# First weights split in halves and a reordered start in a two-layer hybrid decoder trunk

## The reference

```
for l in range(2):
    h = rmsnorm(x, norm_mix[l])
    u, sq, sk, sv, dq, dk, dv, gate_logits = split(h @ w_in[l])
    y_ssm = GLU(gelu(s5_ssm(u, ssm_lam_re[l], ssm_lam_im[l], ssm_log_dt[l], b, c, d)))
    y_sb  = stick_breaking_attention(sq, sk, sv)
    y_da  = differential_attention(rope(dq), rope(dk), dv)
    x = x + (sum of sigmoid(gates) * branch projections) @ w_out[l]
    x = x + cross_attention(rmsnorm(x), rmsnorm(mem)) @ w_xo[l]
    x = x + square(relu(rmsnorm(x) @ w_up[l])) @ w_down[l]
return rmsnorm(x, norm_final)
```

## Time and profile before

| | |
|---|---|
| three runs | 1027.1 us median (1026.31 to 1028.13) |
| the profiled execution | 1026.68 us, its span 1025.0 us |
| TensorE matmul busy | 990.7 us, 97% of the span |
| TensorE weight load busy | 877.4 us, 86% |
| VectorE busy | 765.7 us, 75% |
| ScalarE busy | 550.5 us, 54% |
| mean granted clock | 0.998 |
| HBM read | 176.67 MB |

### The profile page before, as it was taken

One profiled execution on the slowest core, in us unless ns is written; L12 is line 12 of the kernel. 1 busy time (PEld: TensorE's weight loads), 2 busy tenths in 40 slices (PEclk: granted clock), 3 DMA queues, 4 the chain that ended last, 5 costly groups with the idle time before them and its releaser, 6 DMA issues. The chain is left out here.

```text
span 1025.0 us, 17644 instructions
## 1 busy us (share of the span) xinstructions
PE 990.7 (97%) x6784; PEld 877.4 (86%) x6784; DVE 765.7 (75%) x1185; ACT 550.5 (54%) x843; POOL 46.2 (5%) x104
## 2 busy tenths in 40 slices
PE   6999999999999999999999999999999999999996
PEld 6977899999897888888889779999988878888885
DVE  5988997888765866889765569787887567666665
ACT  7455436475755645544464663545656565444543
POOL 5004000000000004000000110000000000000000
PEclk9999999999999999999999999999999999999999
DMA  8797438556644666686657853465665446666661
GB/s 330 240 187 181 124 104 268 147 169 182 182 145 123 247 187 185 195 222 190 195 145 203 178 149 100 142 197 149 180 181 167 141 127 188 191 193 189 185 190 78
DMA packets 64163, 181.37 MB, mean 177 GB/s; under 512 B 19728, under 2 KB 21776, under 8 KB 63440
## 3 DMA queue, kind: packets, MB, share of 16 engines
q1 hardware_dynamic: 63648, 179.91, 60.6%
q10 hardware_dynamic: 432, 0.32, 0.1%
HBM read 176.67 MB, written 3.54 MB: 176 GB/s over the span
## 5 line engine op out<-in xcount | busy, mean ns | idle before, releaser
L1288 DVE TENSOR_TENSOR s_w_lo<-s_raw,s_w_hi 128x1024 fp32r<-128x1024 f32 x312 | 374.9, 1228 | 95.4 <-ACT s_w_hi L914 91.6
L914 ACT ACTIVATE s_w_hi<-s_raw 128x1024 fp32r<-128x1024 f32 x312 | 320.8, 1054 | 183.1 <-PE p_T L1876 76.7
L1874 PE MATMUL p_T<-s_hT,s_w_hi 128*128 128x256 f32 x576 | 165.8, 288 | 0.7 <-ACT s_w_hi L914 0.7
L1875 PE MATMUL p_T<-s_hT,s_w_hi 128*128 128x256 f32 x576 | 162.9, 283 | 0.0
L1876 PE MATMUL p_T<-s_hT,s_w_lo 128*128 128x256 f32 x576 | 162.8, 283 | 0.0
L1874 PE MATMUL p_A<-s_w_hi,s_bT_hi 128*128 128x512 f32 x320 | 125.1, 391 | 2.5 <-DVE s_bT_lo L1288 2.5
L1876 PE MATMUL p_A<-s_w_hi,s_bT_lo 128*128 128x512 f32 x320 | 124.7, 390 | 0.0
L1875 PE MATMUL p_A<-s_w_lo,s_bT_hi 128*128 128x512 f32 x320 | 124.6, 389 | 0.0
L1874 PEld LDWEIGHTS p_T<-s_hT,s_w_hi 128*128 128x128 f32 x576 | 110.2, 191 | 4.6 <-issue 2.7
L1875 PEld LDWEIGHTS p_T<-s_hT,s_w_hi 128*128 128x128 f32 x576 | 110.3, 192 | 0.1
L1876 PEld LDWEIGHTS p_T<-s_hT,s_w_lo 128*128 128x128 f32 x576 | 110.3, 192 | 0.0
(11 more groups left out here) (269 smaller groups left out, 1844.1 us busy)
## 6 DMA issues: line engine op xcount, KB each, us to landing
s_raw<-in_weights SPq DMA_DIRECT2D x312, 512.0 KB, 3.7
s_bt<-in_ssm_bt SPq DMA_DIRECT2D x2, 1024.0 KB, 7.3
s_gates<-f_turn SPq DMA_DIRECT2D x16, 128.0 KB, 7.5
s_x<-in_x SPq DMA_DIRECT2D x1, 1024.0 KB, 10.0
s_dv<-in_ssm_bc SPq DMA_DIRECT2D x2, 512.0 KB, 8.6
u_turn<-s_st_y SPq DMA_DIRECT2D x4, 256.0 KB, 4.7
s_uB<-u_turn SPq DMA_DIRECT2D x16, 64.0 KB, 5.1
s_bt<-in_mem SPq DMA_DIRECT2D x1, 1024.0 KB, 7.0
```

The lines of the kernel that those rows point to most:

```text
L914: return nc.scalar.activation(o, i, f, **kw)
L1288: return V.tensor_tensor(o, i0, i1, op)
L1874: mm(o, lhi, rhi, start=first, stop=False, **kw)
L1875: mm(o, lhi, rlo, start=False, stop=False, **kw)
```

## The change

Four edits belong to the start of the first layer:

- the load of c0 becomes two loads of 256 KB with semaphores of their own, and its hi and lo are made in two halves of 512 columns; TensorE starts when the first halves are there, and waits for the second ahead of the third of the chunk's four row blocks
- the queue of ScalarE issues `col` first, then the first and the second quarter of `x_t` (the second was in SyncE's queue), then the positions
- GpSimd fills `ones` first and the two large zero tensors last; TensorE multiplies `ones` by `ones` nine times (128 columns) into a bank that is not yet in use
- ScalarE prepares c2 and c3 ahead of `p_dt`, and c4 and c5 ahead of `p_cos`; VectorE prepares c2 and c3 ahead of its part of `p_angle` and c4 and c5 ahead of `p_ct`; `rope_angles` moves from the end of `norm` into `p_cos`

The fifth moves `mm_f` and `p_f` from behind units 2 and 3 to behind units 3 and 4, and with them the DMAs of `turn_f` from c15 and c18 to c18 and c21.

```diff
-F_AT = [15, 18, ...]
+F_AT = [18, 21, ...]
-        pre(0, dict(ct=-1, f=(2, 3), cv=(3, 4), b0=5, 
+        pre(0, dict(ct=-1, f=(3, 4), cv=(3, 4), b0=5, 
...
-                return list(range(AHEAD)) if l == 0 else []
+                return list(range(AHEAD + 1)) if l == 0 else []
             n = l * NU + u + AHEAD
-            return [n] if n < DEPTH * NU else []
+            return [n] if AHEAD < n < DEPTH * NU else []
...
+                if g == 0:
+                    load(slot[:, 0:2, :], src[:, 0:2, :], first_landed)
+                    whole = slice(2, None)
+                sp.dma_start(slot[:, whole, :], src[:, whole, :]).then_inc(raw_landed[g % LO], 16)
...
-                    if l == 0 and c == 0:
-                        load_x_t(1)
...
-            nc.gpsimd.memset(kt[:, :, :], 0.0).then_inc(zeroed, 1)
-            nc.gpsimd.memset(bN0[:, :, :, :], 0.0).then_inc(zeroed, 1)
             cst = Steps(consts_made)
+            nc.gpsimd.memset(ones[:, :], 1.0).then_inc(*cst.mid())
...
+            act.dma_start(col[:, :], a["col"][0]).then_inc(prm_landed.sem, 16)
             act.dma_start(x_t[:, X_PARTS[0], :], a["x_t"][:, X_PARTS[0], :]).then_inc(xt_landed[0].sem, 16)
-            act.dma_start(col[:, :], a["col"][0]).then_inc(prm_landed.sem, 16)
+            act.dma_start(x_t[:, X_PARTS[1], :], a["x_t"][:, X_PARTS[1], :]).then_inc(xt_landed[1].sem, 16)
...
+                            if i < 2:
+                                c = slice(512 * i, 512 * i + 512)
+                                act.wait_ge(*((raw_landed[0], 16) if i else st.at(first_landed, 1)))
+                                fn(w_hi[0][:, c], raw[0][:, c]).then_inc(...)
+                            else:
+                                prep_chunk(1)
...
-                        if s in (("p_angle", 0), ("p_cos", 0)):
-                            prep_chunk(2 + (s[0] == "p_cos"))
-                            n_first = AHEAD
+                        if s in (("p_dt", 0), ("p_cos", 0)):
+                            prep(1 + (s[0] == "p_cos"))
+                            n_first = len(nxt)
...
-                        rope_angles()
                         return
...
                 def p_cos(t):
                     n = angles(t)
+                    if t == 0:
+                        rope_angles()
+                        dve.wait_ge(*st.mine())
...
                         if s in (("p_angle", 0), ("p_ct", 0)):
-                            prep_chunk(2 + (s[0] == "p_ct"))
-                            n_first = AHEAD
+                            prep(1 + (s[0] == "p_ct"))
+                            n_first = len(nxt)
...
+            pe.wait_ge(consts_made, 1)
+            for _ in range(9):
+                mm(bank["X0"][:, 0:P], ones[:, :], ones[:, :], start=True, stop=True)
             pe.wait_ge(consts_made, 8)
...
+                                if g == 0 and (k, ft) == (2, 0):
+                                    pe.wait_ge(hi_made.sem, 1)
+                                    pe.wait_ge(lo_made.sem, 1)
```

More of the change, by code:

```diff
@@ L128 @@
 END = 640
-F_AT = [15, 18, 2 * (AT_UNIT["up", 0, 0] + 13) + 11, 2 * (AT_UNIT["up", 0, 0] + 13) + 14]
+F_AT = [18, 21, 2 * (AT_UNIT["up", 0, 0] + 13) + 11, 2 * (AT_UNIT["up", 0, 0] + 13) + 14]
 MIDWAY = []
@@ L483, in hybrid_trunk @@
         free = {b: counted(f"{b}_free", len(USES[b]), credit=1) for b in BANKS}
+        first_landed = counted("first_landed", 1, step=16)
+        first_hi, first_lo = counted("first_hi", 1), counted("first_lo", 1)
         raw_landed = [sem(f"raw_landed{i}") for i in range(LO)]
@@ L646, in _, with load @@
         def _(sp):
+            def load(dst, src, landed):
+                landed.made += 1
+                sp.dma_start(dst, src).then_inc(landed.sem, 16)
             def load_chunk(g):
@@ L649, in load_chunk @@
                     sp.wait_ge(chunk_done.sem, g - LO + 1)
[L650 to L654, removed]
+                slot, src, whole = wslot(raw[g % LO][:, :], g % NC // 2), chunk_src(g), slice(0, None)
+                if g == 0:
+                    load(slot[:, 0:2, :], src[:, 0:2, :], first_landed)
+                    whole = slice(2, None)
+                sp.dma_start(slot[:, whole, :], src[:, whole, :]).then_inc(raw_landed[g % LO], 16)
             def load_params(t):
@@ L800, in _ @@
                                           base=0, pattern=[[-1, P]], channel_multiplier=1).then_inc(*cst.mid())
+            nc.gpsimd.memset(kt[:, :, :], 0.0).then_inc(zeroed, 1)
+            nc.gpsimd.memset(bN0[:, :, :, :], 0.0).then_inc(zeroed, 1)
             pool.wait_ge(*cst.mine())
@@ L914, in fn @@
                 return nc.scalar.activation(o, i, f, **kw)
+            act.dma_start(col[:, :], a["col"][0]).then_inc(prm_landed.sem, 16)
             act.dma_start(x_t[:, X_PARTS[0], :], a["x_t"][:, X_PARTS[0], :]).then_inc(xt_landed[0].sem, 16)
-            act.dma_start(col[:, :], a["col"][0]).then_inc(prm_landed.sem, 16)
+            act.dma_start(x_t[:, X_PARTS[1], :], a["x_t"][:, X_PARTS[1], :]).then_inc(xt_landed[1].sem, 16)
             act.dma_start(stat[:, 62:64].bitcast(I32), a["positions"]).then_inc(pos_landed, 16)
-            xt_landed[0].made += 1
-            prm_landed.made += 1
+            for landed in xt_landed[0:2] + [prm_landed]:
+                landed.made += 1
             act.wait_ge(pre_dve, 1)
@@ L967, in norm @@
                         for i, part in enumerate(X_PARTS):
-                            if i != 1:
-                                prep_chunk(i // 2)
+                            if i < 2:
+                                c = slice(512 * i, 512 * i + 512)
+                                act.wait_ge(*((raw_landed[0], 16) if i else st.at(first_landed, 1)))
+                                fn(w_hi[0][:, c], raw[0][:, c]).then_inc(*(st.sig(hi_made, 1) if i else st.sig(first_hi)))
+                            else:
+                                prep_chunk(1)
                             act.wait_ge(*st.at(prm_landed, 1))
@@ L1385, in norm @@
                         for i, part in enumerate(X_PARTS):
-                            if i != 1:
-                                prep_chunk(i // 2)
+                            if i < 2:
+                                c = slice(512 * i, 512 * i + 512)
+                                dve.wait_ge(*(st.at(hi_made, 1) if i else st.at(first_hi, 1)))
+                                tt(w_lo[0][:, c], raw[0][:, c], f32(w_hi[0][:, c]), ALU.subtract)\
+                                    .then_inc(*(st.sig(lo_made, 1) if i else st.sig(first_lo)))
+                            else:
+                                prep_chunk(1)
                             for k in range(part.start, part.stop):
@@ L1927, in unit @@
                             pe.wait_ge(*st.at(*w))
-                        pe.wait_ge(hi_made.sem, g + 1)
-                        pe.wait_ge(lo_made.sem, g + 1)
+                        if g == 0:
+                            pe.wait_ge(*st.at(first_lo, 1))
+                        else:
+                            pe.wait_ge(hi_made.sem, g + 1)
+                            pe.wait_ge(lo_made.sem, g + 1)
                         wh, wl = wslot(w_hi[g % HI][:, :], u), wslot(w_lo[g % LO][:, :], u)
```

1 line of the change is left out of this document (removed).

## The result

The changed kernel takes 1033.65 us, the median of eight runs (1031.16 to 1036.47); the kernel before took 1026.80 us in the eight runs beside them (1026.31 to 1028.13). The ratio is 1.0062 with a 95% interval of 1.0053 to 1.0072: 6.9 us slower. The execution that was profiled took 1035.49 us, with a span of 1033.8 us, so 8.8 us of span are to be explained in it; the other seven show that some of that comes and goes.

What follows compares the result with a forecast made beforehand. Bound: the places where TensorE waits (start, c6, `mm_k`) and who comes last there. 2.15 (c6) + 2.0 (c25) = 4.15 on the profiled 1026.68 gives 1030.8; the median stands 0.4 higher, so 1031.2; range 1025.8 to 1034.0.

Steps and rivals of the forecast that it cites:

- rival D: At c6: TensorE falls back to half rate after the longer idle time; +1.4 us, time 1032.6; chance 0.08.
- c25: Weight load near 87 us: lands late behind the moved `f_turn` and the `uB` reads; 0 to 3.5 us, taken as 2.0.
- The main term: At c6: the new table order makes TensorE begin it at 32.6 instead of 30.47; +2.15 us.
- The order of the tables: Start of first layer: `p_dt` waits behind c3 until 15.72, squares begin at 23.35 instead of 21.20; +2.15 us at c6.
- more than 2 us idle ahead of it: Sign of being right: ScalarE idles this long before hi c3 at 14.6, released by the DMA.
- The bound of +2.6: At c6: upper bound of the delay, if more queue entries and smaller packets make c3 land later.
- Rival C: Start: c3 lands before hi c2 ends at about 12.4, squares at 21.1; -0.1 us, time 1027.0; chance 0.12.
- The front: Start: first matmul near 7.2 instead of 9.14, 2.4 us gained at c2, all lost in waits by c6.
- my upper bound of 7.0: Start: latest time at which ScalarE could start on the first activations; 5.8 was taken, about 4.5 the earliest.
- The cover of `mm_f`: Ahead of `mm_k`: the 0.81 us wait absorbs `mm_f`'s 0.44 us in TensorE's stream; net 0, without cover +0.44.
- The prediction's third place: `mm_k` at 55.86: TensorE waits 0.81 us for VectorE's work, so this place moves with c6.
- the distance from c6 to `mm_k` not 25.4 us as before: Sign of being wrong: TensorE's own work, not VectorE's chain, would bind there and the front gain would count.

Runs made afterwards that it cites:

- e6: The kernel before with only the new order of the first tables; 1030.83 us, ratio 1.0034.
- e10: The kernel before with VectorE's ten small phase operations (`p_ph0`) moved from behind unit 0 to behind unit 6; 1025.51 us, ratio 0.9987.
- e5: The kernel before with only the fifth edit (f stages one unit later, their DMAs three chunks later); 1029.50 us, ratio 1.0025.
- e9: The kernel before with the front edits and `p_ph0` moved from unit 0 to unit 6; 1025.55 us, ratio 0.9986.
- e11: The changed kernel with the 1 MB load of `x` issued behind c3 instead of ahead of it; 1031.37 us, ratio 1.0042.
- e1: The changed kernel with `mm_f`, `p_f` and the `f_turn` DMAs put back where they were; 1030.48 us, ratio 1.0031.
- e4: The changed kernel with twelve more products of `ones` in TensorE's idle time ahead of c6; 1030.65 us, ratio 1.0035.
- e12: The changed kernel with the f stages and their DMAs put back, `p_ph0` moved to unit 6 and `x` loaded behind c3; 1025.91 us, ratio 0.9990.
- e2: The changed kernel with the old order of the first tables put back; 1029.15 us, ratio 1.0012.
- e7: The kernel before with only the front edits (split c0, queue order, fill order, nine products); 1028.53 us, ratio 1.0013.
- e3: The changed kernel without the nine products of `ones`; 1032.52 us, ratio 1.0044.

## Why the prediction was right and where it was not

It said slower, by 4.1 us, between 1025.8 and 1034.0; the median came out slower by 6.9, at 1033.65. That is inside by 0.35 us, near the end that I had put at rival D with c25 at its worst, and the profiled execution (1035.49) lies outside. The main term was right and came about as it was told. In the profiled execution the distance to the forecast is mostly the half rate, which I had as a rival of 0.08, and the 1.5 us at 527, which I had nowhere.

**The order of the tables: right, 0.7 too small.** Forecast +2.15 at c6, measured +2.89 in after and +2.6 in e6 alone. By its own steps: hi c3 was put at 14.6 with "more than 2 us idle ahead of it", and came at 15.25: +0.6. Whether the changed loads have a part in it cannot be told: with the old loads ScalarE began it at 14.63, 14.68 (e10), 14.94 (e6) and 15.35 (e5), with the new ones at 14.96 to 15.36 in six executions (in e9 at 15.63, where it had landed at 15.4 and ScalarE was late itself). I took one execution's landing, an early one, for the landing. From `p_dt` to the reciprocal I took the old 1.88 us; it took 18.87 - 16.56 = 2.3: +0.4. VectorE's angles were 0.2 quicker than I had them. Together +0.8, and from the squares on the old intervals held to 0.05. The bound of +2.6 was thus a little low. Rival C hung on c3 at 12.4, which e11 shows would have needed the 1 MB of `x` out of the way; and there the squares still came at 22.3, not at 21.1.

**The front: gone, as forecast, but smaller.** I expected the first matmul at 7.2 and starts 0.12 apart from the beginning. Timeline of the start of after:

```profile
1.69 3.89 PE L1879 MATMUL p_X<-s_ones 128*128 128x128 f32 x18 [1.69 <-POOL s_ones L789]
8.64 0.55 PE L1893 MATMUL p_A<-s_hT,s_w_hi 128*128 128x256 f32 x1 [3.07 <-DVE s_hT L1404]
...
4.18 0.63 ACT L918 ACTIVATE s_w_hi<-s_raw 128x512 fp32r<-128x512 f32 x1
6.93 0.91 ACT L918 ACTIVATE s_hT<-s_st_y,s_col 128x256 fp32r<-128x256 f32 x2 [2.12 <-DMA s_st_y<-in_x_t]
```

and a stage of it (columns as above):

```profile
8.00:10.00 2.00, 1.35 (x6) 1.39 (x7) 1.62 (x4) 1.47 (x4) 0.00 (x0) 0.63 1.04 409
```

The half of c0 was there at 4.2, and the quarter of `x_t` at 6.9: putting `col` ahead of it did not bring it near the 5.8 I took, and my upper bound of 7.0 was the true value. The products end at 5.6 and 3.07 us of idle time follow. The trace has the clock at full from 5.1, at half again from 8.5 and at full from 11.9 (the matmul at 11.55 above takes 0.41 us, the one at 12.09 takes 0.28). So the products did raise the rate, and it was lost again before the first real matmul. They do not even do that always: full rate was granted near 5 to 6.5 in after, e1, e4, e11 and e12, and in e2, e7 and e9 only from 11.1, 13.8 and 14.0. The front gained 1.32 at c1 to c3 instead of 2.4, and all of it was gone at c4, where lo c4 was late. In e7, e9 and e12, with the same front, nothing of it comes through at c6 either.

**Rival D: given 0.08, and it happened on top.** The prediction priced it at 1.4 and set it against the forecast; it was an addition to it. The price, 24 x 0.09 = 2.2, was not far off: the rate stayed low from 32.4 to 39.2, a little beyond c6, which cost 2.6. With `mm_f`, and less the 0.76 given back near 50 us, the two come to 2.4, where I had 1.4 and 0. The weight is what failed: against it I held that "the longest unbroken idle time here is 2.6", and for it a fall 4.4 us behind the last matmul. The runs show falls behind 1.9 us (e7), 2.2 (e2) and 3.1 (after, e3, e11) of unbroken idle time, and none behind 0.74 (before) or 2.72 (e6, in the execution profiled). e1 has the same idle time as e6 at the same place, with the same small matmuls ahead of it, and there the clock was at the lower level from 33.3 on:

```profile
33.11 0.37 PE L1893 MATMUL p_T<-s_hT,s_w_hi 128*128 128x256 f32 x1 [2.73 <-issue]
```

The length of one gap alone does not decide it, and a short burst like the 0.71 us of `row` does not prevent it. The Trainium skill (TensorE: Matmul & The Clock Gate, Part 1: The HAM clock gate) has the rule that the throttled level is the default and that an engine which goes idle falls back to it; after and e4 agree with it, by 0.50 against 1.00 in the same stages; e6 shows that an idle time of 2.72 us can also pass without a fall. That rule, cited in the prediction, deserved more than 0.08 once the idle time at c6 had been forecast at 4.7 us with a small burst in it.

**The cover of `mm_f`: nearly right in sum, wrong in place.** I let the 0.81 us of wait ahead of `mm_k` cover it. That wait stands in after with 0.80, in e10 with 0.8 and in e6 with 0.8, whatever VectorE does: it is not a wait for VectorE and covers nothing. What gave back was the wait of 0.47 at 49.83 in before,

```profile
49.83 0.50 PE L1874 MATMUL p_T<-s_w_hi,s_hT 128*128 128x512 f32 x1 [0.47 <-DVE s_qk L1569]
```

which is gone in after and e10. In e4 and e5, where `mm_f` adds its 0.55 at full rate, 0.44 comes back here; in after 0.76 came back of `mm_f` and the half rate together. The prediction's third place should have been this one; "the distance from c6 to `mm_k` not 25.4 us as before" was named as a sign of being wrong, and it was: 61.13 - 33.35 = 27.8, the half rate and `mm_f` less those 0.76.

**c25: right in size for this execution (2.0 forecast, 2.05 measured), with another mechanism, and so by luck.** I let the reads of `f_turn` push c22 to c24 back and c25 with them. The loads before it did come in time; c25 was issued late, because SyncE was held for 8.2 us by eight issues. Two more sizes were off and cancelled: the `f_turn` reads went out at 65.6 and not at 62.5, and c22 landed 14.2 us behind the first of them instead of 17.3, so that 79.8 was met (79.7). c25 landed at 91.9, beyond the 90.3 I had as the latest, and ScalarE was ready for it at 88.2 and not at 86.8. That a late c25 is paid in full holds: ScalarE's wait less the 1.64 it stood there anyway is what TensorE loses, 2.07 in after, 0.5 in e3 (2.11), 0.6 in e2 (2.22) and 1.0 in e11 (2.68). It is no constant: in the profiled executions of e4 and e5 ScalarE does not wait for it at all. A range of 0 to 3.5 was the right thing to write.

**What was in no term**: the 1.5 us at 527. It appears in the profiled executions of after and e11 and in none of the other eleven, at a place where TensorE stands still for 1.3 us in every version. The two groups of runs of the kernel before, told above, lie as far apart, so that it need not come of the change; whether the change makes it likelier is open.

The sum for the profiled execution: 2.9 (c6) + 2.6 (rate) + 0.55 (`mm_f`) - 0.8 (given back) + 2.05 (c25) + 1.5 (527 us) = 8.8 of 8.8. For the medians, the parts alone give 1.4 (e7) + 3.7 (e6) + 2.4 (e5) = 7.5 of 6.9: they add up within what they are known to.

## What to carry to other kernels

Before a start is made quicker, find the next place where the engine waits, and what that place hangs on: here one chain of small operations (parameter tables, statistics, phases) set c6, and moving ten of them off it was worth more than the whole new front. On TensorE an idle microsecond can cost close to two (3.1 of wait and 2.6 of half rate in after), as the clock falls behind it; look at the granted clock right behind every gap that a forecast makes longer, and price the fall as a term and not as a rival. Small reads that fill a queue delay what is *issued* behind them as well as what lands, and a load that is just in time may show in the spread of the runs before it shows in one profile.

## What was not expected of the hardware

- SyncE's time to issue the same eight 64 KB reads: with the `f_turn` reads in the old place 4.9 to 5.3 us in six executions and 7.1 in one (e9), in the new place, 6.3 us ahead of them, 6.8 to 8.2 in six.
- Nine products raised the granted clock at 5.1 us, and 3.07 us of idle time lost it again (half from 8.5); twelve inside an idle time of some 3 us kept it at full (e4).
- The clock fell behind 1.9 us of idle time in e7 and not behind 2.72 in e6. It stayed low for 3.4 us in e1, e2, e7 and e11 (1.5 us lost each) and for 6.8 in after (2.6 lost) and e3 (2.3 lost). Behind 2.73 us in e1 it fell, behind 2.72 in e6 it did not.
- One load of the start, behind the same bytes, landed between 14.6 and 15.4 us in different executions.
